# Reorderings at four places of a two-block transformer kernel: attention scaling, a convolution and two norms

## The reference

```python
# first block, window attention: probabilities of 8 heads in 2 groups of 4
logits = jnp.where(valid, logits + bias, -jnp.inf)
mx = jnp.maximum(logits.max(-1, keepdims=True), sink)
p = jnp.exp(logits - mx)
probs = p / (p.sum(-1, keepdims=True) + jnp.exp(sink - mx))
out = jnp.einsum('bnhgqk,bnkhd->bnqhgd', probs, vb)
...
x = layer_norm(ALPHA * x + h, ln3_g, ln3_b)          # third norm, end of the first block

# second block
h = rms_norm(x, g_pre_mix) * (1 + scale1) + shift1
(sc_b, sc_c, sc_x, q, k, v, z, xbc, dt_raw, gl_a, gl_b, gl_c) = split_columns(h @ w_in)
xbc = silu(causal_depthwise_conv(xbc, conv_w) + conv_b)
...
mix_out = merged @ w_o
x = x + gate1 * rms_norm(mix_out, g_post_mix)         # the mixer's norm
h2 = rms_norm(x, g_pre_ffn) * (1 + scale2) + shift2
gt, up = jnp.split(h2 @ w_ffn_in, 2, axis=-1)
f = (silu(gt) * up) @ w_ffn_out
x = x + gate2 * rms_norm(f, g_post_ffn)
```

## Time and profile before

| | |
|---|---|
| median of 3 runs | 886.11 us (886.01 to 888.78) |
| the profiled execution | 886.01 us, its span 884.2 us |
| PE busy | 852.1 us (96%), 6396 records |
| DVE busy | 650.8 us (74%) |
| ACT busy | 482.7 us (55%) |
| mean granted clock of TensorE | 0.973 of full |
| read from memory | 164.62 MB, 188 GB/s over the span |

### The profile page before, as it was taken

The page is one execution under the profiler, slowest core; times in us unless marked ns, Lnnn a source line. Parts: engine busy times, 40 slices in busy tenths (PEclk is TensorE's granted clock), DMA queues, the critical chain, the costliest instruction groups (busy, mean ns, idle before and its releaser), DMA issues.

```text
span 884.2 us, 15825 instructions
## 1 busy us (share of the span) xinstructions
PE 852.1 (96%) x6396; PEld 805.5 (91%) x6396; DVE 650.8 (74%) x1011; ACT 482.7 (55%) x708; POOL 7.6 (1%) x17
## 2 busy tenths in 40 slices
PE   8999999999999999999997999999998999999997
PEld 7889987989889999999996999898998899999885
DVE  5787797767667888887867896787797866665553
ACT  5643456554547666655546636566547654444452
POOL 0200000000000000000000000000000000000000
PEclk9999999979988999999998999999998899999999
DMA  9986658837143765558852555475564376775751
GB/s 335 246 262 212 212 173 257 255 107 238 45 147 99 222 186 186 176 197 264 267 193 72 162 161 153 155 234 162 190 205 153 95 256 218 225 234 183 176 189 48
DMA packets 139592, 166.89 MB, mean 189 GB/s; under 512 B 5520, under 2 KB 123280, under 8 KB 139520
## 3 DMA queue, kind: packets, MB, share of 16 engines
q1 hardware_dynamic: 137712, 162.82, 58.4%
q0 software_dynamic: 720, 2.02, 1.2%
q10 hardware_dynamic: 1088, 1.05, 0.3%
HBM read 164.62 MB, written 1.25 MB: 188 GB/s over the span
## 4 chain that ended last, share of the span: by engine, by line
PE 62%; DVE 16%; ACT 6%; issue 3%; DVEq 0%; ACTq 0%
PE ps L520 61%; DVE lor L1612 6%; DVE FA L1612 3%; DVE FA L1615 2%; ACT hir L1105 2%; DVE FA L1618 1%; DVE raw L1629 1%; ACT FA L1298 0%; DVE FA L2295 0%; DVE X L1615 0%; ACT FA L1231 0%; DVE X L1612 0%; ACT FA L1491 0%; PE ps L762 0%; ACT L1120 0%
## 5 line engine op out<-in xcount | busy, mean ns | idle before, releaser
L1612 DVE TENSOR_TENSOR lor<-raw,hir 128x1024 fp32r<-128x1024 f32 (+1 forms) x267 | 309.7, 1177 | 108.0 <-ACT hir L1105 105.7
L1105 ACT ACTIVATE hir<-raw 128x1024 fp32r<-128x1024 f32 (+1 forms) x257 | 260.2, 1032 | 119.6 <-PE ps L520 111.5
L520 PE MATMUL ps<-INH,hir 128*128 128x256 f32 (+1 forms) x1064 | 306.7, 288 | 4.2 <-ACT INH L1273 2.5
L520 PE MATMUL ps<-INH,lor 128*128 128x256 f32 (+1 forms) x1064 | 302.5, 284 | 2.9 <-DVE lor L1612 2.9
L520 PE MATMUL ps<-INL,hir 128*128 128x256 f32 (+1 forms) x1064 | 302.9, 285 | 1.1 <-DVE INL L1612 0.9
L520 PEld LDWEIGHTS ps<-INH,hir 128*128 128x128 f32 x1064 | 204.6, 192 | 7.3 <-issue 5.8
L520 PEld LDWEIGHTS ps<-INH,lor 128*128 128x128 f32 x1064 | 204.3, 192 | 5.1 <-DVE lor L1612 4.0
L520 PEld LDWEIGHTS ps<-INL,hir 128*128 128x128 f32 x1064 | 203.8, 192 | 2.1 <-DVE INL L1612 2.0
L520 PE MATMUL ps<-HIH,hir 128*128 128x256 f32 x688 | 197.5, 287 | 0.0
L520 PE MATMUL ps<-HIH,lor 128*128 128x256 f32 x688 | 194.5, 283 | 0.8 <-DVE lor L1612 0.8
L520 PE MATMUL ps<-HIL,hir 128*128 128x256 f32 x688 | 193.8, 282 | 0.0
(11 more groups left out here) (271 smaller groups left out, 772.2 us busy)
## 6 DMA issues: line engine op xcount, KB each, us to landing
raw<-in_w_in SPq DMA_DIRECT2D x64, 512.0 KB, 4.6
raw<-in_mod_wT SPq DMA_DIRECT2D x48, 512.0 KB, 4.4
raw<-in_ffn_w_up SPq DMA_DIRECT2D x44, 512.0 KB, 4.5
raw<-in_w_ffn_in SPq DMA_DIRECT2D x44, 512.0 KB, 4.6
raw<-in_w_ffn_out SPq DMA_DIRECT2D x22, 512.0 KB, 4.6
raw<-in_ffn_w_down SPq DMA_DIRECT2D x20, 512.0 KB, 4.7
raw<-in_xa_wkv SPq DMA_DIRECT2D x16, 512.0 KB, 4.5
raw<-in_xa_wq SPq DMA_DIRECT2D x8, 512.0 KB, 4.9
```

What stands on the lines that cost most here:

```text
L520: return e.matmul(o, l, r, start=start, stop=stop, skip_group_check=True)
L1105: e.activation(hi, src, ACT.Copy).then_inc(*w_hi.up(i))
L1612: return e.tensor_tensor(o, a, b, op)
```

## The change

There are four places. Nothing is computed in another way; instructions are moved.

- **Window attention, DVE.** In `swa(1)` one yield stands ahead of the scaling of the probabilities instead of behind it, so one more step of the filler is issued ahead of it.
- **Second block, DVE.** The convolution of the unit `bc` (`xbc(2)`) stands ahead of the splits that go with `scc`, not behind them.
- **Third norm, PE.** The four sums over the last two tiles of `X` stand behind two steps of `q`/`k`, not behind one.
- **Mixer's norm, DVE and PE.** The splits that go with `wo` 3 stand ahead of the last product of `mix e`; the two branches on single tiles stand behind the small steps for `rm2`, the second one behind its reciprocal; on PE the broadcast of `mix r` stands behind the sums for `mix y`. The branch no longer waits for `mix f 3`, which stands ahead of that broadcast on PE.

```diff
@@ tensor
             mm.mark("h1 free")
             g = late_g([("q", 2), ("k", 2)], xg, 4)
-            steps_of(g, 1)
+            steps_of(g, 2)
             w.wait_ge(dve.at(("n3", "x", 3)))
             for m in range(2):
                 for i in range(2):
                     column(Y3[:, m, 0:3], X[:, 6 + i, :], m, MV[:, i, :])
-            steps_of(g, 1)
             w.wait_ge(act.at("n3 sq 3"), act.at("n3 qg 3"))
...
-            spread_bank("mix r", rm)
             w.wait_ge(dve.at("mix e 3"))
...
             t.then_inc(*mm.up("mix y"))
+            spread_bank("mix r", rm)
             spread_bank("mix r2", rm2)
@@ vector
                 yield 2 * g
                 yield 1
+                if g:
+                    yield 1
                 w.wait_ge(act.at(("exps", g)))
...
                 yield 1
-                yield 1
+                if not g:
+                    yield 1
...
+            xbc(2, split=False)
+
             ahead.unit(("scc", 2), 8)
-            xbc(2, split=False)
-
...
-                if c == 2:
+                if c > 1:
                     ahead.unit(("wo", c), 8)
...
             e.reciprocal(rm, sm0).then_inc(*dve.up(("mix r", "factor")))
-            ahead.unit(("wo", 3), 8)
-            br, br2 = bank["mix r"], bank["mix r2"]
-
-            def branch(k, n):
-                d, xc = MO[:, k:k + n, :], X[:, k:k + n, :]
-                w.wait_ge(mm.at("mix r"), act.at("mix f 3"), act.at(("out", ("unit", ("wo", 3)))))
...
-            branch(0, 1)
-            branch(1, 1)
             w.wait_ge(mm.at("mix y"))
...
+            branch(0, 1)
             w.wait_ge(act.at("mix root"))
             e.reciprocal(rm2, pm).then_inc(*dve.up(("mix r2", "factor")))
+            branch(1, 1)
```

More of the change, by code:

```diff
@@ L2368, in vector @@
             e.reciprocal(rm, sm0).then_inc(*dve.up(("mix r", "factor")))
-            ahead.unit(("wo", 3), 8)
-            br, br2 = bank["mix r"], bank["mix r2"]
-            def branch(k, n):
-                d, xc = MO[:, k:k + n, :], X[:, k:k + n, :]
-                w.wait_ge(mm.at("mix r"), act.at("mix f 3"), act.at(("out", ("unit", ("wo", 3)))))
-                tt(d, d, over(br[:, 0:T], n), MUL).then_inc(*dve.up(("out", "mix r")))
-                then("d")
-                tt(xc, d, xc, ADD).then_inc(*dve.up(("mixed", k)))
-            branch(0, 1)
-            branch(1, 1)
             w.wait_ge(mm.at("mix y"))
@@ L2392, in vector, with branch @@
             ts(pm, pm, RMS_EPS, None, MAX).then_inc(*dve.up("mix square mean"))
+            br, br2 = bank["mix r"], bank["mix r2"]
+            def branch(k, n):
+                d, xc = MO[:, k:k + n, :], X[:, k:k + n, :]
+                w.wait_ge(mm.at("mix r"), act.at(("out", ("unit", ("wo", 3)))))
+                tt(d, d, over(br[:, 0:T], n), MUL).then_inc(*dve.up(("out", "mix r")))
+                then("d")
+                tt(xc, d, xc, ADD).then_inc(*dve.up(("mixed", k)))
             def scaled(k, n):
```

## The result

The changed kernel takes 892.88 us in the median of 4 runs (890.99 to 893.64), beside 886.06 for the kernel before (884.98 to 888.78); the ratio is 1.0066, with an interval from 1.0045 to 1.0087. All 18 executions of the changed kernel on record, the profiled one among them, go from 890.03 to 896.13 us, with a median of 892.2. The kernel is slower, as forecast: by 2 us more than forecast in the median, and by 1 us more by the ratio. One execution, of the kernel with place C alone, took 2109 us, and its ratio leaves that one out. The profiled execution of the changed kernel took 890.62 us with a span of 888.8. The sum of the prediction (890.8) starts from the profiled execution of before, so I hold it against this one, which is one of the faster ones.

What follows compares the result with a forecast made beforehand. PE, 62% of the chain and gapless over long stretches, was taken to bound the kernel. From 886.01 us, terms of +2.7, +1.7, -0.5 and +0.9 gave 890.8 us, with a range of 887.4 to 893.4.

Steps and rivals of the forecast that it cites:

- place C: Third norm's column sums: running them behind the second q/k step removes a PE stall, gain 0.5 us (0.3 to 0.55).
- The sum: Profiled time before plus the four places' terms: 886.01 + 2.7 - 0.5 + 1.7 + 0.9 = 890.8 us.
- second rival: Window attention: the clock falls at PE's 2.7 us gap, costing 2.5 us more, 893.3 us in all; chance 0.12.
- Place A: Window attention: DVE's scaling comes later, so PE's second group of transposes starts 2.7 us later; cost 2.7 us.
- fourth rival: Window attention: DVE need not wait for ACT, cost 1.6 instead of 2.7 us, 889.7 us; within the forecast's 0.60.
- Place B: Convolution of `bc` ahead of two splits: PE waits for the low half of `scx` chunk 4; cost 1.7 us.
- Place D: Mixer's norm: later product, 16 column passes at 1.2 GHz, first scaled product 0.9 us later; cost 0.9 us.
- first rival: Mixer's norm: passes and broadcasts run at the high clock, sums take 1.8 us, -1.2 us there, 888.7 us; chance 0.12.
- third rival: Low-clock restarts behind first, second and mixer's norm get shorter, returning about 7 us, at the extreme 883.8 us; chance 0.16.

Runs made afterwards that it cites:

- C_apart: The changed kernel with one step of q and k (12 matmuls) put between the 128x3 and 128x1 sums of the third norm: 890.46 us, ratio 1.0037.
- the filled norms: The kernel before with 16 extra matmuls of 256 columns, results thrown away, in PE's waits in each of the first two norms: 886.48 us, ratio 0.9997.

## Why the prediction held, and where it did not

The time of 892.88 us lies in the stated range. It lies above the forecast's own bounds (888.9 to 892.4), in the part that the range held open for the second rival, and the clock did fall at A in one of the two traces of the changed kernel.

- **Place A**: 2.7 forecast, 2.67 of idle time and 2.8 in the ledger. The view that carried it is the plain order of DVE beside the one ACT row; the fourth rival (DVE not waiting) is refuted by the 1.13 us in the row. The second rival, that the clock falls there, came true in two of five traces and cost 1.6 us instead of 2.5.
- **Place B**: 1.7 forecast, 1.7 in the ledger. But alone it moved the time by 1.2 us at most. What the step lacks is that the time of before holds falls of the clock elsewhere, and that work moved by 1.7 us can miss them.
- **Place C**: the failed step is "So the whole stage comes forward. Gain: 0.5 us". The gain needs the 24 matmuls between sums and broadcast to run at 0.12 us, and I had not asked what 128x3 and 128x1 passes side by side do to the clock, though I asked just that for D and A. With the clock up it is 0.56; with it down it is -1.0, and down it was in both traces of the changed kernel. That the narrow passes side by side are the cause is likely and not proved (2 of 3 traces against none of 11). A rival "the clock falls behind the sums at C", +1.5 us, was missing.
- **Place D**: 0.9 forecast, 0.95 in four traces (alone, both of the changed kernel, changed without C) and 1.6 in `C_apart`. The 1.2 GHz level of the passes, taken from the earlier trace rows, was right in all of them. The sums took 3.4 us, not the 1.8 us of the first rival. The rule of the Trainium skill (TensorE: Matmul & The Clock Gate, section LDWEIGHTS (loading the stationary operand)), which has no term for the level of the clock, agrees at the high level (0.11 us a pass) and is not borne out at the low one, where a pass took 0.21 us in each of these five traces.
- **The sum** met the profiled execution, since C's error (+1.5) and the fall at 618 that the trace of before had and this one has not (-1.5) cancel, and the 0.8 us won behind the second norm is partly set off by small delays elsewhere. That the sum came out within 0.2 us is luck. The median is 2 us above the sum. The fall at A, 1.6 us in the second trace, would take an execution there, but how many of the 18 hold it is not known, and the kernel before's own spread is as large.
- **The third rival** (restarts shorter by up to 7 us) was mis-sized. Its mechanism is there: behind the second norm the clock rose sooner after the restart and 0.8 us came back. Its size is not: the filled norms show that with the low clock cut from 10 to 3 us a norm returns 0.7 to 1.3 us, since DVE's low halves are next. Its chance of a time at or under 886 was too high. (Half of its 7 us would leave 887.3, not 887.4.)

## What to carry to other kernels

Where one engine's stream is gapless and in order, read the last use of each moved result there, and price an edit by how much later that result is ready: this gave three of four places to 0.1 us. Before crediting an edit for taking a wait out, ask what now stands side by side on PE: narrow column sums with no wider matmuls between them cost more in clock here, in two of three traces, than the wait did. Before crediting or blaming an edit for the difference of two profiled executions, list the low stretches of both: one fall more or less is worth as much as these edits. And a low clock is worth recovering only up to the next producer: look at what PE would wait for if it were faster.

## What was unexpected of the hardware

The same gap or the same passes don't always bring the clock down: the 1.7 us of idle time at 617 us was followed by about 3 us at 1.2 GHz in 4 of 14 traces, the 2.7 us at A in 2 of 5. Such a stretch costs about half its length where PE sets the pace. The instant counts: the fall at 617 came in 4 of 5 traces with this work at its old time or sooner, and in none of 9 with it 1.5 to 6.8 us later. What else decides it between executions of one program is not shown by these runs.
